# Rotated queries and keys turned by a trip through memory and VectorE, and six weight matrices stored block by block

## The reference, cut to what matters

```python
u = h @ w_in
q_r, k_r, v_r, z_r, q_a, k_a, v_a, m_r, m_a = split(u)
qr = rotary(q_r, pos) * (R_DK ** -0.5)           # 8 heads of 128
kr = rotary(k_r, pos)
# retention_chunk, per head
scores = einsum('bihd,bjhd->bhij', q, k) * dmask
o = einsum('bhij,bjhv->bihv', scores, v) + einsum('bihd,bhdv->bihv', q, S) * cross
S_new = S * decay + einsum('bjhd,bjhv->bhdv', k * kdec, v)
y = (sig(m_r) * (yA @ w_br_ret) + sig(m_a) * (yB @ w_br_att)) @ w_out
x = x + g1 * y;  x = x + g2 * (relu(h2 @ w_up)**2 @ w_down)
```

## Time and profile before

| | |
|---|---|
| median of 3 runs | 1806.72 us (1802.99 to 1807.86) |
| profiled execution, its own time | 1803.19 us |
| its span | 1801.2 us |
| mean granted TensorE clock | 0.998 of full speed |
| PE busy | 1782.5 us (99%) |
| DVE busy | 994.8 us (55%) |
| ACT busy | 736.0 us (41%) |
| POOL busy | 353.4 us (20%) |
| DMA | 505240 packets, 348.47 MB, mean 193 GB/s |

### The profile page before, as it was taken

How to read it: one execution, slowest core, us unless ns; L and a number is a source line. 1 busy time by engine, 2 the same in 40 slices (tenths; PEclk the granted TensorE clock), 3 DMA queues, 4 the chain that set the end, 5 groups by cost and what they waited for, 6 DMA issues and landing times.

```text
span 1801.2 us, 35393 instructions
## 1 busy us (share of the span) xinstructions
PE 1782.5 (99%) x11933; PEld 1624.8 (90%) x11933; DVE 994.8 (55%) x1606; ACT 736.0 (41%) x1411; POOL 353.4 (20%) x459
## 2 busy tenths in 40 slices
PE   8999999999999999999999999999999999999998
PEld 7888888889999999999988888888899999999998
DVE  5466666667433575543364666666674346655333
ACT  3444444446222344532234444444463234554222
POOL 3333333330000120000023334333300004000000
PEclk9999999999999999999999999999999999999999
DMA  9878898896666734455638779888865635344432
GB/s 343 232 200 215 225 239 231 231 236 199 210 211 208 260 95 127 129 177 200 218 104 237 204 215 230 231 224 240 231 220 165 211 118 199 117 128 125 132 125 99
DMA packets 505240, 348.47 MB, mean 193 GB/s; under 512 B 201931, under 2 KB 468109, under 8 KB 505110
## 3 DMA queue, kind: packets, MB, share of 16 engines
q1 hardware_dynamic: 484992, 292.13, 56.3%
q0 software_dynamic: 12592, 44.99, 7.7%
q10 hardware_dynamic: 7526, 9.58, 1.5%
HBM read 313.56 MB, written 34.37 MB: 193 GB/s over the span
## 4 chain that ended last, share of the span: by engine, by line
PE 97%; DVE 1%; ACT 1%; issue 1%; ACTq 0%; POOL 0%; DVEq 0%
PE G L1591 50%; PE G L1627 32%; PE X L1752 8%; PE X L1650 2%; PE X L1551 2%; PE G L1861 2%; PE X L1627 1%; DVE wlo L1093 0%; PE X L1644 0%; DVE hp L1164 0%; DVE rstd L1154 0%; ACT hp L791 0%; ACTq L766 0%; ACT whi L772 0%; DVE hlo L1169 0%
## 5 line engine op out<-in xcount | busy, mean ns | idle before, releaser
L1093 DVE TENSOR_TENSOR wlo<-raw,whi 128x1024 fp32r<-128x1024 f32 x369 | 471.0, 1277 | 546.0 <-ACT whi L772 543.9
L772 ACT ACTIVATE whi<-raw 128x1024 fp32r<-128x1024 f32 x369 | 390.9, 1059 | 761.8 <-PE G L1591 442.3
L1627 PE MATMUL G<-whi,hhi 128*128 128x512 f32 x832 | 333.9, 401 | 1.7 <-DVE hlo L1169 1.4
L1627 PE MATMUL G<-whi,hlo 128*128 128x512 f32 x832 | 325.0, 391 | 0.0
L1627 PE MATMUL G<-wlo,hhi 128*128 128x512 f32 x832 | 324.5, 390 | 0.1
L1591 PE MATMUL G<-hhi,whi 128*128 128x384 f32 x704 | 236.8, 336 | 0.0
L1591 PE MATMUL G<-hhi,wlo 128*128 128x384 f32 x704 | 235.4, 334 | 0.0
L1591 PE MATMUL G<-hlo,whi 128*128 128x384 f32 x704 | 235.3, 334 | 0.0
L1627 PEld LDWEIGHTS G<-whi,hhi 128*128 128x128 f32 x832 | 156.2, 188 | 49.2 <-issue 13.1
L1591 PE MATMUL G<-ysp,whi 128*128 128x384 f32 x768 | 196.9, 337 | 0.0
L1627 PEld LDWEIGHTS G<-wlo,hhi 128*128 128x128 f32 x832 | 156.1, 188 | 34.1 <-DVE wlo L1093 0.6
(11 more groups left out here) (237 smaller groups left out, 2545.3 us busy)
## 6 DMA issues: line engine op xcount, KB each, us to landing
raw<-in_w_in_dram SPq DMA_DIRECT2D x256, 128.0 KB
raw<-in_w_in_dram SPq DMA_DIRECT2D x128, 256.0 KB
raw<-in_w_up_dram SPq DMA_DIRECT2D x64, 512.0 KB
raw<-in_w_down_dram SPq DMA_DIRECT2D x64, 512.0 KB
raw<-in_w_in_dram SPq DMA_DIRECT2D x49, 512.0 KB
ada_w<-in_w_ada_dram SPq DMA_DIRECT2D x44, 512.0 KB, 6.1
kc<-in_cache_attn_k_dram SPq DMA_DIRECT2D x64, 256.0 KB, 6.7
vc<-in_cache_attn_v_dram SPq DMA_DIRECT2D x32, 512.0 KB, 7.5
```

The costliest lines, as they stand in the source:

```text
L772: return a.activation(out, in_, ACT.Copy)
L1093: v.tensor_tensor(wlo[:, j % SPLIT, :, :], raw[:, j % RAW, :, :], whi[:, j % SPLIT, :, :].bitcast(F32), ALU.subtract).then_inc(blk_split, 1)
L1627: ins = t.matmul(B[banks[m][0]][:, :], x[:, kp * WK + k, m * P:(m + 1) * P], w[:, k, :], start=first and k == 0 and x is hhi and w is w_hi ...
```

## The change

Three things. First, the six weight matrices are no longer inputs of their own: one input `w_blk` holds all 368 blocks in the order in which they are used, each as 128 rows of 1024 numbers, laid out by numpy before the launch. A load is one DMA with 4 KB for each partition. Second, the rotated queries and keys are no longer turned on TensorE: SP stores `qkR` into `rq_d` in memory (one DMA, `rotated_out`), reads it back with its 32x32 squares in place (four DMAs, `rotated_back`) into the new tile `rkT`, and DVE turns the squares (`rotated_turned`). `qrT`, `krT` and their copies out of PSUM are gone; the score products read `rkT`. Third, `keys_low` and `qr_par` move from the end of a head's list on DVE to behind block 1 of the next head.

```diff
+def blocks(w_in, w_br_ret, w_br_att, w_out, w_up, w_down):
+    ...
+    return np.stack(out)
...
-            for src in parts:
-                w = src.shape[-1]
-                ...
-                sp.dma_start(dst[:, :, off:off + w], src.rearrange("(k p) n -> p k n", p=P))\
-                    .then_inc(raw_full[j % RAW], 64 // len(parts))
+            sp.dma_start(raw[:, j % RAW, :, :].rearrange("p k n -> p (k n)"),
+                         w_blk[bass.ds(n, 1)].rearrange("a p n -> p (a n)")).then_inc(raw_full[j % RAW], 64)
...
+        def rotated_out(c, l, h):
+            sp.wait_ge(rope_ready, c.head)
+            sp.dma_start(rq_d[bass.ds(l * HEADS + h, 1)].rearrange("s a p d -> p (s a) d"),
+                         qkR[:, :, :].rearrange("p t (a d) -> p (t a) d", a=2)).then_inc(rq_out, 16)
+        def rotated_back(c, l, h):
+            sp.wait_ge(rq_out, c.head * 16)
+            for m in range(4):
+                src = rq_d[bass.ds(l * HEADS + h, 1), :, :, 32 * m:32 * m + 32]
+                sp.dma_start(rkT[32 * m:32 * m + 32, :, :].rearrange("j a (q i) -> j (a q) i", i=32),
+                             src.rearrange("s a (q j) i -> j (s a q) i", j=32)).then_inc(rk_full, 16)
...
                 for j in range(4):
-                    load(c, j, [pair_rows(l, j, h * DH + base, DH) for base in (C_QA, C_KA, C_QR, C_KR)], wide)
+                    if prev is not None and j == 3:
+                        rotated_out(c, l, prev)
+                    load(c, j, h * 8 + (l * BLOCKS + B_HEAD + j))
+                if prev is not None:
+                    rotated_back(c, l, prev)
                 sp.wait_ge(ss_done, c.head)
...
# ScalarE
-            act.wait_ge(tr_done, H + 1)
-            copy(krT[:, :], X[1][:, 0:TOK]).then_inc(kr_ev, 1)
...
# VectorE
+        def rotated_turned(c):
+            dve.wait_ge(rk_full, c.head * 64)
+            tiles = rkT[:, :, :].rearrange("p a t -> p (a t)")
+            v.transpose(tiles, tiles).then_inc(rk_turned, 1)
+            dve.wait_ge(rk_turned, c.head)
+            dve.wait_ge(dec_full, c.head * 16)
+            row = dec[:, DC_ROW:DC_ROW + 64].rearrange("p (g t) -> p g t", g=4)
+            c.op(v.tensor_tensor(par(qr_par[:, 0, :], 0), par(rkT[:, 4, :], 0), row, ALU.mult))
+            v.tensor_tensor(par(qr_par[:, 1, :], 1), par(rkT[:, 4, :], 1), row, ALU.mult).then_inc(qr_ev, 1)
...
             low(c, 1)
             if prev is not None:
+                rotated_turned(c)
+                keys_low(c)
                 probabilities(c)
                 decayed(c)
...
-            dve.wait_ge(tr_done, H + 1)
-            dve.wait_ge(dec_full, H * 16 + 16)
-            c.op(v.tensor_copy(qrT[:, :], X[0][:, 0:TOK]))
-            ...
-            keys_low(c)
...
# TensorE
-            pe.wait_ge(qr_ev, c.head)
-            pe.wait_ge(kr_ev, c.head)
-            mm(X[0][:, 0:256], krT[:, 0:P], qrT[:, 0:2 * P])
-            ...
+            pe.wait_ge(rk_turned, c.head)
+            mm(X[0][:, 0:256], rkT[:, 1, :], rkT[:, 0:3:2, :])
+            ...
-            pe.wait_ge(rope_ready, H + 1)
-            for n in range(NT):
-                turned(X[0][:, n * P:(n + 1) * P], qkR[:, n, 0:DH])
-            for n in range(NT):
-                ins = turned(X[1][:, n * P:(n + 1) * P], qkR[:, n, DH:2 * DH])
-            ins.then_inc(tr_done, 1)
```

More of the change, by code:

```diff
@@ L80, in tables, with rows, pair_rows @@
     return np.ascontiguousarray(rope, np.float32), dec.astype(np.float32)
+def blocks(w_in, w_br_ret, w_br_att, w_out, w_up, w_down):
+    def rows(w, l, k, c):
+        return w[l, k * BK * P:(k + 1) * BK * P, c:c + BC].reshape(BK, P, BC).transpose(1, 0, 2).reshape(P, BK * BC)
+    def pair_rows(l, k, parts, n):
+        return np.concatenate([w_in[l, k * WK * P:(k + 1) * WK * P, c:c + n].reshape(WK, P, n) for c in parts], axis=2)\
+            .transpose(1, 0, 2).reshape(P, WK * WC)
+    out = []
+    for l in range(DEPTH):
+        out += [pair_rows(l, j // 2, (C_VA + j % 2 * WC,), WC) for j in range(8)]
+        for h in range(HEADS):
+            out += [pair_rows(l, j, [h * DH + base for base in (C_QA, C_KA, C_QR, C_KR)], DH) for j in range(4)]
+            out += [pair_rows(l, j, [h * DV + base for base in (C_VR, C_ZR)], DV) for j in range(4)]
+        for i in range(2):
+            for g in range(2):
+                for w, base, ks in ((w_in, C_MR, 2), (w_in, C_MA, 2), (w_br_att, 0, 2), (w_br_ret, 0, 4)):
+                    out += [rows(w, l, k, i * (2 * BC) + (base + g * BC)) for k in range(ks)]
+        out += [rows(w_out, l, j % 2, i * (2 * BC) + j // 2 * BC) for i in range(2) for j in range(4)]
+        out += [rows(w_up, l, j // 2, j % 2 * BC) for j in range(4)]
+        out += [rows(w_up, l, j % 2, i * (2 * BC) + j // 2 * BC) for i in range(1, 8) for j in range(4)]
+        out += [rows(w_down, l, j, i * BC) for i in range(4) for j in range(8)]
+    return np.stack(out)
 def plan(groups):
@@ L251, in trunk @@
     kaT = sb("kaT", [P, TOK], stack=hstack)
-    qrT = sb("qrT", [P, SEQ + P], stack=hstack)
-    krT = sb("krT", [P, TOK], stack=hstack)
+    rkT = sb("rkT", [P, 2 * NT, P], stack=hstack)
     vaT = sb("va_tok", [P, NT, AW], stack=hstack)
@@ L501, in head @@
                                  src.rearrange("l b (n j) h i -> j (l b n h) i", j=32)).then_inc(kc_full, 16)
-                load(c, 4, [pair_rows(l, 0, h * DV + base, DV) for base in (C_VR, C_ZR)], wide)
+                load(c, 4, h * 8 + (l * BLOCKS + B_HEAD + 4))
                 sp.wait_ge(ss_read, c.head)
@@ L506, in head @@
                 for j in range(1, 4):
-                    load(c, 4 + j, [pair_rows(l, j, h * DV + base, DV) for base in (C_VR, C_ZR)], wide)
+                    load(c, 4 + j, h * 8 + (l * BLOCKS + B_HEAD + 4 + j))
                 sp.wait_ge(pv_done, c.head)
@@ L537, in _ @@
                     for j in range(4):
-                        load(c, j, [rows(w_out, l, j % 2, i * (2 * BC) + j // 2 * BC)])
+                        load(c, j, l * BLOCKS + B_OUT + i * 4 + j)
                         if i:
@@ L557, in _ @@
                     for j in range(8):
-                        load(c, j, [rows(w_down, l, j, i * BC)])
+                        load(c, j, l * BLOCKS + B_DOWN + i * 8 + j)
                         if l < DEPTH - 1 and j == DOWN_SENT[min(i, 1)]:
```

75 lines of the change are left out of this document (34 added, 41 removed).

## The result

The changed kernel takes 1865.38 us (median of four runs, 1855.73 to 1867.76) against 1805.23 for the kernel before on the same chips: a ratio of 1.033, 95% interval 1.030 to 1.035. It is slower by 60 us. The forecast was 1795.5; the second rival named the right side and the right place, and priced it at 1826.

A forecast was written before the change was run, and what follows sets the result against it. PE bounds the kernel, busy 1782.5 of 1801.2 us. Removal 11.3 less waits 1.6 gives 9.7 us, so 1793.5 from the profiled execution, 1797.0 from the median, 1795.5 between; range 1789 to 1800, overall 1788 to 1831.

The forecast's parts named there:

- the second rival: Reads in the heads share engines with POOL's next states' loads; PE waits 1.4 to 3 us a head, about 1826; chance 0.24.
- The removal: PE in each head loses the six turns of `qkR`: 0.705 us a head, 11.3 us in all.
- the layout: Weights in blocks, one DMA a load on SP: saves nothing directly, makes room on SP and the DMA engines.
- DVE's 1.8 us of slack: DVE's longer list behind block 1 finishes the scores' rest part at 283.1; PE wants it at 284.9.
- the third rival: DVE's longer list or its held turn makes PE wait, about 0.5 us a head beyond the wait, around 1810; chance 0.03.
- The deadline: Data for DVE's turn must land by 278.1 for PE's score products at 279.1 in the fifth head.
- The loads ahead of the store: Three loads in SP's queue, 1.57 MB at 352 GB/s, take 4.5 us, to 269.6.
- The store beside the states: The store of `qkR` gets stuck behind POOL's new states to 273.3, landing at 274.3.
- the first rival: The store waits out the states' whole transfer, reads come 0.4 to 1.1 us late; 1800 to 1811; chance 0.15.
- The reads: Four SP reads issued 0.6 us apart, the last at 276.2, landing 2.0 us later at 278.2: PE waits 0.1 us a head.
- The cliff: A read issued later than about 276.7 meets POOL's states' loads and lands 1 to 3 us late.
- the side without a wait: The forecast itself: PE waits under 0.4 us a head in the heads, 1789 to 1800; chance 0.58.

The follow-up runs named there:

- run 2: The changed kernel without the store and reads, DVE turning the squares of `qkR` where they are; 1791.39 us, ratio 0.9934.
- run 1: The kernel before with only the block layout of the weights, one transfer a load; 1803.82 us against 1803.16, ratio 1.000.
- run 12: The changed kernel with POOL issuing the states' store only after the store of `qkR` has landed; 1863.65 us, ratio 1.032.
- Run 7: The changed kernel without the store, its four reads taking the same pattern from the input states; 1819.57 us, ratio 1.008.
- run 8: The changed kernel with 14 unused products on PE ahead of its wait for `rk_turned`; 1857.06 us, ratio 1.0285.
- Run 15: The order of run 13 with the store of `qkR` issued by ACT instead of SP; 1795.31 us, ratio 0.9944.
- run 13: The changed kernel with loads 0 and 1 ahead of the `y_ret` transfers, loads 2 and 3 behind store and reads; median 1805.99 us, ratio 1.002.
- run 17: A third profile of the unchanged kernel of run 13; the profiled execution took 1803.89 us.
- run 3: The changed kernel with the store of `qkR` issued on ACT's queue, reads still on SP; 1899.47 us, ratio 1.054.
- run 5: The kernel of run 3 with the weights in their old layout, four transfers a load; 1936.55 us, ratio 1.073.
- run 9: The changed kernel with loads 0 and 1 ahead of the `y_ret` transfers, store and reads ahead of load 3; 1804.23, 1825.72, 1822.41 and 1795.25 us against 1805.18.

## Why the prediction was wrong, step by step

In short: two terms of the chain were too small, a load ahead of the store (1.5 us of the engines, measured 2.2) and the landing of a read (2.0 us, measured 4.6), and the price of a wait lacked the slow clock behind it (21 us in all).

**The removal.** 11.3 us forecast, 12 measured by run 2. Right. So was the layout at nothing (run 1), and DVE's 1.8 us of slack: the third rival never appeared.

**The deadline.** Right: in the one head of the changed kernel where data landed before rotation end + 12.1 PE didn't wait, and those at + 12.5 to + 13.0 cost it 0.4 us, but for one with 1.9.

**The loads ahead of the store.** In the chain this step is the first that failed: "so a load is about 1.5 us of all 16 engines". I took 352 GB/s from the best 2.5 us of the head, in which POOL's single store had nearly all of the time. The three loads took from 272.5 to 279.0 in the fifth head:
```profile
272.50:279.00 6.50, 6.50 (x43) 4.94 (x42) 4.26 (x7) 2.37 (x8) 3.78 (x6) 1.00 0.95 257
```
257 GB/s in all, the loads 2.2 us each. That is 6.5 us in place of 4.5 ahead of the store, and 233 GB/s stood for the old loads in the row above the one that I used. I put that rate down to the issues and the short pieces; the load with long pieces isn't much faster.

**The store beside the states.** I had it landed 8.7 us after the rotation's end. It is + 8.1 to + 12.5 from the third head of a layer on, in all but one, + 9.1 in the median. So the place came out, the mechanism only in part. I had the store held by the states in every head. Its first piece moved 4.5 to 5.5 us after the issue in eleven of the twelve heads, behind the loads, and run 12, with no transfer of the states beside it, still has it landed at + 8.0 to + 10.6. The states decide in five heads, in which it landed at + 11.0 to + 12.5 here and at + 8.4 to + 9.2 in run 12; these five hold 31 of the 49.7 us of waits. The states' store is longer too, 9.8 us in the median for 6.7, half of it from the blocks alone (8.2 in run 1), and its load comes later.

Two workings of the prediction were wrong by themselves, whatever was measured. A transfer of 2.0 us with 0.3 for its bytes and 0.8 ahead of them leaves 0.9 behind the last byte; I gave the store 0.3, and with 0.9 the last read would have landed 0.7 us past the deadline, which is the first rival. And by equal turns the states' 16 pieces an engine leave the store 16 turns of its 48, a third of it, and not all.

**The reads.** This is the term that cost most in the ordinary head: "a small transfer lands 2.0 us after its issue". That is `y_ret`, 48 KB at a quieter time. The trip's reads take 4.6 us in the median, from 2.3 to 8.2:
```profile
DMA to landing us min/median/max: 2.3/4.6/8.2
```
Each head lost about 2.6 us here, which by itself turns a wait of 0.1 us into one of 2.7. From the third head of a layer on, the last read leaves at rotation end + 11.0 in the median, where I had + 10.6, and lands at + 15.4, where I had + 12.6. Run 7 shows the same without any store: last landing at + 13.7 to + 14.9 in these heads. In the first head of each layer, which has no states' store and no load just ahead, the store landed at + 3.3, 5 us ahead of the forecast, and the last read still at + 12.5.

**The cliff.** The second rival set it at a read issued later than 276.7, which is rotation end + 11.1. Five heads are beyond it, with waits of 3.5 to 9.6 us, 31 us together. But the heads that issued their last read before it, from the third on, waited 1.9 to 3.2 us too, for the reads' own slowness. The rival's price, 1.4 to 3 us a head, lies just under the mean (49.7 / 16 = 3.1); its sum of 20.7 was for 2.

**The clock.** Not in the prediction at all, in no rival: 21 us. With it the second rival would have stood at 1847. A price for a wait of PE has to carry it, and run 8 shows that it hangs on PE's idling.

In the chances: slower had 0.27, and a chain of five steps with a margin of 0.1 us at its end didn't bear 0.58 for the side without a wait. Run 15 and two of the three profiled runs of 13 show what the forecast described, 1794 to 1796. What these have in common is loads 0 and 1 issued well ahead of the store (7 us in the fifth head of run 15), loads 2 and 3 behind the reads, and a states' store that is never out more than 0.2 us ahead of the trip's.

## What to carry to other kernels

A transfer that something waits for is priced from what its queue and the other queues hold when it is issued, at the rate that such transfers had in that stretch, not at the best rate seen. If its margin is under a microsecond, place it first: issue it from an engine that isn't in a queue of its own work at that moment, and put the large transfers behind it. Where a kernel's executions spread by more than a per cent, suspect a race between two issues, and compare the profiles of two executions head by head.

## What the runs showed of the hardware

- The granted clock falls to half after waits of PE, for 3.4, 6.8 or 10.2 us. In the changed kernel ten waits of 1.9 to 9.6 us did it and two of 2.7 and 2.8 us didn't. In run 17, behind the wait of 6.8 us:
```profile
1127.90:1133.10 5.20, 5.20 (x14) 4.34 (x15) 4.23 (x11) 2.30 (x5) 0.55 (x1) 0.50 1.01 160
```
- A transfer of 512-byte pieces on a queue of its own is held back by large loads that another queue already holds: 0.39 MB took 11.3 us in the median beside loads of 0.5 MB in 4 KB pieces and the states (run 3), 3.9 beside the old loads (run 5), 2.6 to 4.1 with the loads out of the way (run 13).
- In run 9 the small store landed 0.03 us ahead of the states' store that had been issued 0.40 us before it. The Trainium skill (DMA: Bandwidth & Descriptors, section Queues, rings and completion order) says that an engine's completion write lands only after every earlier write of that engine, across its queues. That alone isn't what made the landing late: 90% of the store's 768 pieces had moved 4.8 us after its issue, but the last at 7.0 us, among the states' pieces, and the landing came 0.56 us behind the last one, as in the other heads (0.4 to 0.5). The queues from 269.5 to 272:
```profile
q0 software_dynamic: 213, 0.81, 79.1%
q1 hardware_dynamic: 91, 0.04, 5.8%
```
- The DMA engines have room for the trip, if it is in its place: in the same stretch of 44 us, from 245 to 289, their share is 0.95 in run 15 (first row), with PE never idle, and 0.83 in the changed kernel, with PE waiting.
```profile
245.00:289.00 44.00, 44.00 (x286) 35.91 (x285) 28.73 (x53) 19.23 (x50) 17.16 (x20) 1.00 0.95 250
```
```profile
245.00:289.00 44.00, 41.65 (x269) 33.63 (x268) 23.58 (x40) 18.59 (x49) 16.59 (x19) 0.99 0.83 219
```
